# Block 0's output projection in quarters, its norm ahead of scan step 14, and GLU block 1 behind the first match

## The reference

```
q, k, v, u = split(x @ w_in + b_in)                  # 4 x 512 channels
att  = dilated causal windows (128,1) (512,4) (2048,16), 8 heads, merged by their denominators
y    = S5 scan of u: 64 complex states for each of 32 groups;  y = Re(C h) + D u
z    = gelu(y);  ssm = z * sigmoid(z @ w_glu + b_glu)
h    = LN1(ALPHA * x + concat(rms(att), rms(ssm)) @ w_out + b_out)
PEER: q = h @ w_pq; per head two scores q1 @ keys1, q2 @ keys2; top 16 of each,
      top 16 of the 256 sums, g = softmax of them; sum over 128 experts of g * gelu(h . u[e]) * v[e]
y    = LN2(ALPHA * h + PEER(h) + sigmoid(h @ w_ple_gate) * (p @ w_ple))
```

## Time and profile before

| | us |
|---|---|
| median of 3 runs (1966.63 to 1971.59) | 1967.59 |
| the profiled execution | 1970.92 |
| its span (first to last instruction) | 1969.1 |
| first gather issued by POOL, from the span's start | 269.11 |

### The profile page before, as it was taken

How to read it: one execution, slowest core, us unless ns; L and a number is a source line. 1 busy time by engine, 2 the same in 40 slices (tenths; PEclk the granted TensorE clock), 3 DMA queues, 4 the chain that set the end, 5 groups by cost and what they waited for, 6 DMA issues and landing times.

```text
span 1969.1 us, 23845 instructions
## 1 busy us (share of the span) xinstructions
PE 1476.8 (75%) x7204; PEld 702.5 (36%) x7204; DVE 1348.7 (68%) x3199; ACT 794.1 (40%) x2756; POOL 776.6 (39%) x796
## 2 busy tenths in 40 slices
PE   7999886876785767667775776666856766687987
PEld 6765562332232334334331222222222333322331
DVE  6977977775657778888886754444344467885665
ACT  2132237682422544544444443333333223353554
POOL 0943324343332444454433333233233343454442
PEclk9999987797987989889987888888887788898999
DMA  7012489999999999999999999999999999999997
GB/s 296 1 43 92 162 310 411 356 381 419 391 374 405 409 394 421 421 417 421 408 419 395 400 412 420 421 420 420 422 414 423 422 421 416 400 403 416 401 422 289
DMA packets 100656, 723.17 MB, mean 367 GB/s; under 512 B 11968, under 2 KB 12736, under 8 KB 20416
## 3 DMA queue, kind: packets, MB, share of 16 engines
q0 software_dynamic: 82944, 604.02, 75.2%
q1 hardware_dynamic: 17600, 117.77, 15.0%
HBM read 714.78 MB, written 4.87 MB: 365 GB/s over the span
## 4 chain that ended last, share of the span: by engine, by line
DMA 36%; PE 24%; DVE 14%; ACT 6%; issue 5%; POOL 1%; POOLq 0%; ACTq 0%; DVEq 0%
DMA R<-d_uv,W 36%; PE bank L1353 12%; DVE R L2107 8%; PE bank L1265 2%; PE bank L1132 2%; PE bank L1292 2%; ACT L1624 1%; PE bank L1124 1%; ACT W L1627 1%; POOL R L889 1%; PE bank L1178 1%; ACT W L1632 1%; PE bank L1261 1%; PE bank L972 1%; ACT W L1595 1%
## 5 line engine op out<-in xcount | busy, mean ns | idle before, releaser
L889 POOL DMA_INDIRECT R<-d_uv,W x576 | 670.2, 1164 | 1032.3 <-PE bank L1353 831.3
L1353 PE MATMUL bank<-R,W 128*32 128x512 f32 x2304 | 717.6, 726 | 436.3 <-ACT W L1632 436.2
L2107 DVE CUSTOM_DVE_ANT_0 R<-R,W 128x1024 f32<-128x1024 f32 x576 | 696.8, 1223 | 468.8 <-DMA R<-d_uv,W 465.1
L1353 PEld LDWEIGHTS bank<-R,W 128*32 128x32 f32 x2304 | 198.6, 122 | 829.6 <-ACT W L1632 587.6
L1595 ACT CAST W<-W 128x2 uint32<-128x2 f32 x292 | 55.6, 192 | 899.0 <-DVE W L2107 898.8
L1632 ACT ACTIVATE W<-W 128x32 f32<-128x32 f32 x576 | 153.5, 313 | 9.4
L1627 ACT ACTIVATE W<-W 128x1 f32<-128x1 f32 x576 | 138.2, 287 | 9.5
L933 PE MATMUL bank<-E,W 128*128 128x256 f32 (+1 forms) x384 | 103.5, 428 | 10.2 <-DMA E<-d_xT 8.1
L1292 PEld LDWEIGHTS bank<-E 128*128 128x128 f32 x768 | 90.3, 196 | 25.6 <-issue 25.6
L1292 PE MATMUL bank<-E 128*128 128x128 f32 (+1 forms) x768 | 95.1, 282 | 0.0
L933 PEld LDWEIGHTS bank<-E,W 128*128 128x128 f32 x384 | 75.9, 201 | 31.9 <-issue 10.5
(11 more groups left out here) (315 smaller groups left out, 1712.6 us busy)
## 6 DMA issues: line engine op xcount, KB each, us to landing
E<-d_kc SPq DMA_DIRECT2D x8, 2560.0 KB, 20.9
E<-d_w_pq SPq DMA_DIRECT2D x6, 2048.0 KB, 12.5
E<-d_vc SPq DMA_DIRECT2D x8, 1536.0 KB, 26.5
W<-d_w_pq SPq DMA_DIRECT2D x5, 2048.0 KB, 11.4
R<-d_uv,W POOLq DMA_INDIRECT x576, 12.1
E<-d_w_out SPq DMA_DIRECT2D x4, 2048.0 KB, 12.1
E<-d_vc SPq DMA_DIRECT2D x8, 1024.0 KB, 30.7
W<-d_w_in SPq DMA_DIRECT2D x3, 2048.0 KB, 21.1
```

What stands on the lines that cost most here:

```text
L889: pool.indirect_dma_start(ring[r], None, A["uv"], bass.IndirectOffsetOnAxis(ap=stage[:, half, s:s + 1], axis=0),).then_inc(landed[r], 16)
L1353: last = mm(acc[TG * js[s]:TG * js[s] + TG, half * 512:half * 512 + 512], wsel[:, r, :], ring[r][:, D + half * 512:D + half * 512 + 512], ...
L2107: last = nc.vector.tensor_tensor_reduce(ring[r][:, 0:D], ring[r][:, 0:D], hrep[:, js[s], :], 1.0, 0.0, ALU.mult, ALU.add, dots[:, x, s:s + 1])
```

## The change

In the list:
- `project_first` runs by quarters: both attention quarters at step 12, without the wait for the product of block 0 and for the last piece of v; the two scan quarters at step 13, behind `ssm_out 12` and ahead of `ssm_in 14`.
- `residual` of block 0 is split: `residual_att` at the end of step 13, `residual_ssm` with the statistics, `root` and `normal` ahead of scan 14 (before: behind it).
- `skip_term 13`, `turn` and the first half of `ask(0,0)` follow scan 14; then `ssm_in 15` and the second half.
- `glu_block(1)` and `gate_block(1)` move from step 14 to behind `match(0,0)`, `ssm_out 14` and `ssm_out 15`. `product_rest(1)` moves from ahead of `tops(0,0,0)` to behind `first_stage` and `alpha`.
- SP starts the load of w_pq part 0 after the first scan quarter (a new semaphore, out_left) and part 1 after out_full.

```
@@ order_of_front
-        if n < steps:
+        if n < 14:
             order.append(("scan", n))
...
-        if n in (12, 13):
-            order += following + [("ssm_out", n - 1)] + parts
+        if n == 12:
+            order += following + [("ssm_out", 11), ("project_first", 0, 0), ("project_first", 1, 0)]
+        elif n == 13:
+            order += [("ssm_out", 12), ("project_first", 1, 1), ("project_first", 0, 1)] + following
         elif n == 14:
-            order += [("ssm_out", 13)] + following
-        elif n < 15:
+            order += [("ssm_out", 13), ("residual_ssm",), ("root", 0), ("normal", 0, 0), ("normal", 0, 1)]
+            order += [("scan", 14), ("skip_term", 13), ("turn", 0), ("turn_out", 0), ("ask", 0, 0, 0)] + following
+            order += [("ask", 0, 0, 1)]
+        elif n == 15:
+            order += [("scan", 15)]
+        elif n < 14:
...
         if n == 15:
-            order += [("ask_out", 0, 0), ("match", 0, 0), ("match_out", 0, 0), ("skip_term", 14), ("product_rest", 1)]
+            order += [("ask_out", 0, 0), ("match", 0, 0), ("match_out", 0, 0), ("ssm_out", 14), ("skip_term", 14)]
         if n == steps:
-            order += [("ssm_out", 15), ("tops", 0, 0, 0), ("skip_term", 15)]
+            order += [("ssm_out", 15), ("glu_block", 1), ("gate_block", 1), ("tops", 0, 0, 0), ("skip_term", 15)]
...
+        if n == 13:
+            order.append(("residual_att",))
...
-        if n == 14:
-            order += [("glu_block", 1), ("residual", 0), ("root", 0), ("normal", 0, 0), ("normal", 0, 1), ("skip_term", 13)]
-            order += [("turn", 0), ("turn_out", 0), ("gate_block", 1), ("ssm_out", 14), ("ask", 0, 0, 0), ("ask", 0, 0, 1)]
...
-    order += [("lay", 0, 0, 0), ("lay_too", 0, 0, 1), ("first_stage",), ("alpha",)]
+    order += [("lay", 0, 0, 0), ("lay_too", 0, 0, 1), ("first_stage",), ("alpha",), ("product_rest", 1)]
@@ SP
+            sp.wait_ge(out_left, 1)
+            load(parts_of[0][0], eight(A["w_pq"][0]), in_pq[0])
             sp.wait_ge(out_full, 1)
-            load(parts_of[0][0], eight(A["w_pq"][0]), in_pq[0])
             load(parts_of[0][1], eight(A["w_pq"][1]), in_pq[1])
@@ DVE
+            def residual_att():
+                dve.wait_ge(in_rows1, 16)
+                dve.wait_ge(in_xr, 16)
+                link(stt(hB[0], hB[0], ALPHA, rows1[:, 0, :], ALU.mult, ALU.add))
+                dve.wait_ge(out_att, 1)
+                link(stt(hB[0], bankf[:, 0:D], ssq[:, 0, 0:1], hB[0], ALU.mult, ALU.add))
+
+            def residual_ssm():
+                dve.wait_ge(out_full, 1)
+                stt(hB[0], bankf[:, D:2 * D], ssq[:, 1, 0:1], hB[0], ALU.mult, ALU.add).then_inc(out_used, 1)
```

More of the change, by code:

```diff
@@ L147, in order_of_front @@
         order += [("scores", i) for i in now] + [("bias", i) for i in now] + [("exps", i) for i in now]
-        parts = [("project_first", 2 * (n - 12) + i) for i in range(2)] if n in (12, 13) else []
         wide = [x for x in p if PIECES[x][0] != "v" or n < 11]
@@ L577, in build @@
             sem(n) for n in ("z_ready", "glu_full", "sig_ready", "mixed", "sq_full", "ssq_ready"))
+        out_att, out_left = sem("out_att"), sem("out_left")
         out_full, out_used, var_ready, ln_root, h_ready = (
@@ L1094, in free, with project_first @@
                 pe.sem_inc(slot_free, n)
[L1096 to L1100, removed]
+            def project_first(half, part):
+                if part == 0:
+                    if half == 0:
+                        pe.wait_ge(sc_biased, NH)
+                        pe.wait_ge(at_done, 1)
+                    pe.wait_ge(in_out[half], 16)
+                elif half == 1:
                     pe.wait_ge(mixed, 1)
                     wait_put(pe, len(PIECES) - 1)
-                if part == 0:
-                    pe.wait_ge(in_out[half], 16)
                 for k in range(CT):
@@ L1107, in project_first @@
                               wout_first[half][:, CT * part + k, :], start=(k == 0), stop=(k == CT - 1))
-                if n == 3:
+                if half == 1:
+                    last.then_inc(out_left if part else out_att, 1)
+                elif part == 1:
                     last.then_inc(out_full, 1)
@@ L2036, in put_v @@
                     v_put, 1)
+            def residual_att():
[7 more added lines that the diff above has]
+                stt(hB[0], bankf[:, D:2 * D], ssq[:, 1, 0:1], hB[0], ALU.mult, ALU.add).then_inc(out_used, 1)
+                dve.wait_ge(out_used, 1)
+                spread_of(0)
             def residual(b):
                 _, m = tokens_of(b)
-                rows = rows1 if b < QB else s_rows1
-                n = 0 if b < QB else 1
-                dve.wait_ge(in_rows1, 16 * (1 if b < QB else 3))
+                dve.wait_ge(in_rows1, 16 * 3)
                 dve.wait_ge(in_xr, 16 * (b + 1))
-                link(stt(hB[b][0:m, :], hB[b][0:m, :], ALPHA, rows[0:m, 0, :], ALU.mult, ALU.add))
-                dve.wait_ge(out_full, n + 1)
+                link(stt(hB[b][0:m, :], hB[b][0:m, :], ALPHA, s_rows1[0:m, 0, :], ALU.mult, ALU.add))
+                dve.wait_ge(out_full, 2)
                 link(stt(hB[b][0:m, :], bankf[0:m, 0:D], ssq[0:m, 0, b:b + 1], hB[b][0:m, :], ALU.mult, ALU.add))
@@ L2048, in residual @@
                     ALU.mult, ALU.add).then_inc(out_used, 1)
-                dve.wait_ge(out_used, n + 1)
+                dve.wait_ge(out_used, 2)
                 spread_of(b)
@@ L2160, in _ @@
                      "product_rest": product_rest, "take_sums": take_sums, "rms": rms, "rms_inverse": rms_inverse,
-                     "alpha": alpha, "residual": residual, "residual_half": residual_half, "normal": normal,
+                     "alpha": alpha, "residual": residual, "residual_att": residual_att, "residual_ssm": residual_ssm, "residual_half": residual_half, "normal": normal,
                      "tops": tops, "cross": cross, "put_v": put_v, "resolve": resolve, "lay_too": lay_too, "experts": experts, "gate_out": gate_out,
```

## The result

| | before | after |
|---|---|---|
| median, the two measured side by side | 1970.71 us (10 runs) | 1979.72 us (10 runs) |
| lowest to highest | 1963.32 to 1977.46 | 1971.57 to 1985.09 |
| ratio, 95% interval | | 1.0047 [1.003, 1.0064] |
| the profiled execution, its span | 1970.92, 1969.1 | 1978.3, 1976.5 |
| first gather | 269.11 us | 279.41 us |

What follows compares the result with a forecast made beforehand. Two chains, DVE's and PE's, bound the first gather, and PE's was held to end last: 6.4 us later, plus 1.7 and 0.5 for the clock, gives 8.6 on 1967.6, 1976.2 us; own range 1973.5 to 1979.5, wider range 1969 to 1981.

Steps and rivals of the forecast that it cites:

- h_ready at 224.9, a 0.9 us wait for out_full: On DVE, residual and norm of block 0: a 0.9 us wait, then h_ready at 224.9 us, before 233.6.
- Scan 15 waits 2.7 us for POOL, starts at 234.9: On DVE, scan 15 directly behind scan 14 waits for POOL's carry 14 and runs from 234.9 to 242.2 us.
- rival C: More lost: late w_pq load holds scan 15, or the clock is low twice in the chain; 4 us more, 1981; chance 0.08.
- `ssm_out 15` done at 246.3, DVE idles 2.0 us: Behind the first tops, `skip_term 15` waits for carry 15 and `ssm_out 15`; DVE idles 2.0 us, starting it at 246.3.
- GLU 1, 3.7 us: On PE behind `ssm_out 15`: 16 matmuls of GLU 1 now stand in the chain and add 3.7 us.
- Gap of 2.5 us for the gate: On PE, GLU 2 writes GLU 1's bank and waits for ACT's gate: 2.4 us plus 0.1 us.
- From GLU 2 to the exp's end 18.6 us: On PE and ACT, the work from GLU 2 to the exp's end is unchanged at 18.6 us.
- The clock, 1.7 + 0.5 us: PE's clock low once in the chain behind `ssm_out 15`, 1.7 us; a third of a chance at the attention quarters, 0.5 more.
- The product costs nothing: On DVE, the product's new place delays tops of (0,1) by 2.1 to 4.2 us, covered by idle time before the second dot.
- I pass all 8.6 us on to the end: From first gather to kernel end: last slots and loads shift alike, nothing catches up, so all 8.6 us reach the end.
- A: Rival: the late gathers' time is given back later, result 1967.6 to 1971 us; chance 0.12.
- B: Rival: PE's chain doesn't hold the pick, DVE's decides from 262.6; 1965.5 us, or 1960.8 at its far end; chance 0.10.

Runs made afterwards that it cites:

- After_again: The changed kernel, unchanged, traced and timed a second time against the kernel before: ratio 1.0046.
- glu_only: The kernel before with GLU block 1 and its gate moved behind `ssm_out 15` and the product behind `alpha`; projection and norm as before: ratio 1.0053.
- glu_back: The changed kernel with GLU block 1 ahead of the turn and its gate back where they were: ratio 1.0011 to the kernel before.
- warm: The changed kernel with 12, 4, 14 and 10 useless matmuls filling PE's idle times: ratio 1.0028 to the kernel before.
- product_only: The kernel before with only the product of block 1 moved behind `alpha`: ratio 0.9982.
- exp_first: The changed kernel with ACT's exp of the first pick ahead of `ask(0,1,x)`, and match, `ask_out` and block 3's gate later: ratio 1.0069 to the kernel before.
- glu_bank6: The changed kernel with GLU block 1 writing bank 6, so GLU 2 needn't wait for the gate: ratio 1.0049 to the kernel before.
- both: glu_back with `ssm_in 15`, `ask(0,1,0)` and `tops(0,0,1)` earlier, GLU 3 behind the match and its gate behind `resolve`: ratio 0.9996 to the kernel before.
- both2: The kernel both with the load of fold in the middle of the hrep loads: ratio 0.9975 to the kernel before, repeat 0.9967.
- exp_hold: exp_first with POOL's first gather held until all 16 hrep loads have landed: ratio 1.006 to the kernel before.

## Why the prediction was right, point by point

The forecast was 1976.2 us from a median of 1967.6, that is 8.6 us slower (ratio 1.0044); measured are 1.0047 and 1.0046. The mechanism was right: GLU 1, its gate and GLU 2 in one chain behind `ssm_out 15`. The close number is in part luck. The gather was 10.3 us late and not 8.6, the exp's wait 11.11 us and not 7 to 10, and the measured time (5.9 to 12.6 us by its interval) can't tell these two apart. By its steps:

1. *Attention quarters*, 203.6 to 210.7 at full clock: as forecast (7.1). After_again shows the other end, 9.09.
2. *out_full at 219.1*: 218.8.
3. *h_ready at 224.9, a 0.9 us wait for out_full*: the norm ended at 224.7, the wait wasn't there. The residual took that time itself: L2050 started at 215.30, inside POOL's first product (215.20 to 216.47), and needed 2.25 us and not the 1.22 of L2044; POOL's second product, started inside L2050, took 2.25 and not 1.28. Before, L2044 had started first (225.30, POOL's product at 225.46), and only POOL's product was longer (2.19). The rule that the prediction cites (the Trainium skill, GPSIMD Engine Reference, "Specifications") says that GpSimd and a DVE instruction of two SBUF inputs contend, and the rows agree: L2050 reads two SBUF tiles. The prediction cited the rule for carries 14 and 15 and left it out here, where it cost 1.0 us. Beside the tops carry 15's products took 1.27 each, 2.5 us together, as by the rule, and not the 3.0 of the upper end.
4. *Scan 15 waits 2.7 us for POOL, starts at 234.9*: it waited 3.42 us and started at 235.65, and PE ended the wait, not POOL (whose product ended at 234.54). `ask(0,0,0)` took 6.25 us at clock 0.50 instead of 3.8 and held `ssm_in 15` behind it. That PE would release this gap is the prediction's own sign for rival C, and it came, with another cause: the w_pq load was in time. It cost 0.75 us beyond the forecast, for POOL had covered the rest.
5. *First tops at 242.6*: 243.21, step 4's delay.
6. *`ssm_out 15` done at 246.3, DVE idles 2.0 us*: 247.4 and 2.73. Step 4 adds 0.75 us and `ssm_out 15` at the low clock 0.8 (1.79 where I took 1.0), POOL gives 0.5 back, 0.1 are hand-overs.
7. *GLU 1, 3.7 us*: 4.74, the clock. glu_only shows that this and step 8 are the whole slowdown (1.0053); without them glu_back has none that its interval resolves.
8. *Gap of 2.5 us for the gate*: 2.66. The table load took 1.28 us and the sigmoid started 0.02 us behind it, so the 2.66 us a switch of the other cited rule (the Trainium skill, ScalarE: Activation LUTs, "What ACT_TABLE_LOAD costs") doesn't show here either; that the gap is also 2.66 is chance, since it holds 1.28 of load, 1.14 of sigmoids and 0.24 of hand-over.
9. *From GLU 2 to the exp's end 18.6 us*: 20.16, GLU 2 took 5.44 at the low clock instead of 3.84.
10. *The clock, 1.7 + 0.5 us*: this is the term that was mis-sized. I expected the low level once; it came three times. Against the chain without it (271.1), the exp ended at 274.98, 3.9 us later: 1.1 from steps 4 and 6, 1.0 from step 7, 0.2 from the gap, 1.6 from step 9. The clock's own share is 4.1 (0.75, 0.8, 1.0 and 1.6) where I took 2.2, and POOL's 0.5 takes part of it back. warm removes it and lands at 6.57 against 6.4. So the gather was 10.3 us late, 0.4 beyond the 279 that I named as its last moment. Two sums in the prediction are off by little: the upper end of its own range is 1979.2 by its terms (6.4, 3.7 and 1.5) and not 1979.5, and rival C is 1980.2 and not 1981.

*The product costs nothing*: right, by product_only. Its three instructions took 2.3 us instead of 4.2.

*"I pass all 8.6 us on to the end"*: right in size here, wrong as a rule. Here hrep, the last slots and the gathers did all shift together, by 10.3 us each, and the time followed. exp_first brought the gathers alone 8 us forward (5 behind scan 13), D2 came 3 us later, and no time was won. What decides is when the first two dots can run, and they need hrep as well as rows. Both columns of D2 put the kernels in nearly the order of their times. G does so less well, above all for exp_first, which is the slowest of all with the gather of glu_back (271.83 and 271.88).

*The rivals.* A: the end was late in both measurements; what looks like giving back in the trace happens without the change too. B: the exp, at 274.98, missed its 262.6 by 12 us. C: both of its causes have to be looked at. The gap ahead of scan 15 was released by PE, at 0.75 us, a fifth of its price, and the clock was low three times in the chain. Together they made the gather 1.7 us later than forecast, where C had 4.

What stays open: why glu_bank6 gained 6.6 us at D2 on after_again and nothing in time, and why the clock stays low for 13.7 us at some 340 us in some executions and not in others.

## What to carry to other kernels

Work that is moved off one chain has to be priced on the chain where it lands: GLU 1 filled a hole on PE for nothing, and behind the last thing that the pick waits for it cost its length, the round trip of its only bank, and the low clock behind the gap. Before a big stream is started earlier, ask what else its first consumer needs and which queue carries it: here the earlier gather alone gave nothing, and with half of the loads of hrep put ahead of one late wait on SP the kernel became faster than the one before, though the share of this step isn't resolved. And where single traces of one kernel differ by more than the effect, measure from a common instruction near the edit, and let the repeated runs judge the end.

## What the runs showed of the hardware

- Two traces of one program can stand 8.0 us apart at 390 us in a run of 1970 us, with the lag made in steps (1.4 at 314 us, 5.9 at 366, 8.0 at 387). The steps fall where one of the two had PE at 0.50 (341.8 to 355.5 and 369.1 to 379.3 us) with PE busy, and the other had not.
- In the front, between 215 and 262 us, each of the 18 idle times of PE of 2.66 to 5.76 us in eight of the traces was followed by longer matmuls (the turn 1.34 to 1.97 us instead of 1.09, `ssm_out 15` 1.76 to 1.94 instead of 1.08, GLU 2 5.43 to 5.44 instead of 3.84); 2.26 us ahead of the turn in the earlier trace rows was not. In both and both2 no idle time of PE in that stretch is over 2.2 us, and in warm twelve useless matmuls ahead of the turn kept it at 1.09.
- In six of the 14 traces (after_again, warm, glu_bank6, exp_first, both2 and its repeat) PE itself stalled without a semaphore in the middle of `ask`, with gathers in flight; in the other eight, the first of before among them, it didn't. Timeline of PE in exp_first:

```profile
271.80 6.30 PE L1301 MATMUL bank<-E,W 128*128 128x128 f32 x54
279.14 0.48 PE L1301 MATMUL bank<-E,W 128*128 128x128 f32 x2 [1.04 <-issue]
```

  What held it there no run here tests.
- The 16 loads of hrep took SP 10.1 to 10.4 us to issue in eleven traces, with gathers in flight beside them (10.39, exp_first) or without (10.14, exp_hold), and 11.49 in warm. In both2 and its repeat the two halves took 5.79 and 4.96, 6.37 and 5.02 us.
- DVE's product took 0.68, 0.69 and 0.90 us away from POOL and 1.72, 1.64 and 0.86 beside it.
